# Token groups of 428, 426 and 426 in the down product, and all output blocks turned at its end

## The chip, the cores and the metric

One core of a Trainium2 chip runs the kernel. The metric is the device time of one execution in microseconds, the median of several runs. A profiled execution gives the span from the first to the last instruction, and what each engine did in it.

## The reference

One layer of a hybrid backbone works on 256 context tokens and 1024 latent tokens of 1024 features. After a recurrent branch and an attention branch comes a feed-forward part with a convolution along the tokens, then a last normalisation:

```python
def conv_ffn(h, lp):
    u, gte = jnp.split(h @ lp['w_ffn_up'], 2, axis=-1)
    u = dwconv3(u, lp['conv_ffn'])
    return (jax.nn.gelu(u) * gte) @ lp['w_ffn_down']

    x = x + g2 * conv_ffn(h2, lp)          # in layer(); g2 differs for context and latent tokens
    y_prompt = rmsnorm(xp, norm_f_g)       # in reference()
    y_sample = rmsnorm(xs, norm_f_g)
```

The change concerns the product with `w_ffn_down` (2816 x 1024, called the down product here), the gated addition to x, and the last normalisation. All is float32.

## The kernel before

Features lie on the 128 partitions and tokens along the free dimension; the 1280 tokens are stored with the 256 of the context first. Each float32 product is made of three matmuls of rounded parts (`split_mm`, L1069 to L1071): high part of the weights by high part of the tokens' values, high by low, low by high. The parts are made by the other engines: ScalarE rounds (`activation` with Copy), VectorE and GpSimd subtract the rounded from the whole.

The order of the work on each engine is written out by hand, with semaphores between the engines. The down product runs last. Its input, the gated hidden values (22 blocks of 128 features, `fact_kept`), and x1 (`x1_kept`) have been written to device memory before.

- `DOWN` (L630) lists three groups of tokens, as first token and count. For each group c the kernel goes through the 22 blocks of the hidden dimension; the step j = 22c + k holds 8 output blocks n of 3 matmuls each, 24 matmuls on 128 weights by the group's tokens. Each output block n accumulates over the 22 steps of a group in its own bank of PSUM (2 KB a partition, 512 float32 values); in the group of 256 two blocks share a bank, so that group uses banks 0 to 3 (`down_bank`).
- Operands of a step lie in a ring of three slots. SyncE (SP) loads a step's weights, 512 KB (`load_down`, L1012), and hidden values (`load_fact`, L1020) once PE has ended the step that was three earlier. ScalarE rounds the weights and then the tokens' values (L2215, L2216). GpSimd (POOL) splits the upper half of the weights (L3018); VectorE (DVE) splits their lower half (L2841) and then the tokens' values (L2844, `split_down`). PE waits for all of these (`down_part`).
- At the end of a group VectorE reads the eight banks, multiplies by the gate and adds x1 (`add_down`, L2854). In its own order this stands behind the split of the third step of the next group. PE's first step of a new group waits, block by block, for this add.
- An output block of 128 tokens is then turned by eight transposes on PE into a pair of banks (`turn_y`, L1741); ScalarE squares and sums it and takes the root of the mean (`square_y`, L2207 and L2209); VectorE takes the reciprocal and scales by it and by the gain (`scale_y`, L2860 and L2867) into one of four buffers; SP stores it (`store_y`, L1047). The groups run in the order tokens 256 to 767, 768 to 1279, 0 to 255. So eight of the ten output blocks are ready to be turned while the third group runs; they use banks 4 to 7 then, one in every second step (`y_step`). The last two follow the last add.

Of the kernel before, what the change touches and what calls it, by code (L numbers as in the profile page):

```python
# [22 lines left out]
P = 128  # L23
# [116 lines left out]
def build(nc, dram):  # L140
    ctx = ExitStack()
    with ctx:
# [487 lines left out]
        DOWN = [(256, 512), (768, 512), (0, 256)]  # L630
# [13 lines left out]
        Y_BLOCKS = list(range(2, TB)) + [0, 1]  # L644
# [49 lines left out]

        def y_step(q):

            return 2 * FB + 2 + 2 * q
# [18 lines left out]
        def _(sp):  # L716
# [327 lines left out]
            def store_y(q):  # L1044
                b = Y_BLOCKS[q]
                sp.wait_ge(y_ready, q + 1)
                sp.dma_start(dram["y"][b], y_tok[:, q % 4, :]).then_inc(tiles_moved[q % 4], 16)  # L1047

            for j in range(SLOTS, NSTEP):
                load_down(j)  # L1050
                load_fact(j)
                for q in range(TB - 2):
                    if j == min(y_step(q) + 5, NSTEP - 1):
                        store_y(q)
            for q in range(TB - 2, TB):
                store_y(q)
# [7 lines left out]
        def _(pe):  # L1064
# [643 lines left out]
            def down_bank(c, n):  # L1708

                if c < 2:  # L1710
                    return PS[:, n, 0:512]
                return PS[:, n // 2, 256 * (n % 2):256 * (n % 2) + 256]

            def down_part(j, blocks):

                c, k = j // FB, j % FB
                s, m = j % SLOTS, DOWN[c][1]
                pe.wait_ge(w_split, DOWN_SPLIT + j + 1)
                pe.wait_ge(fact_split, 2 * j + 2)
                for n in blocks:  # L1720
                    if k == 0 and c == 1:
                        pe.wait_ge(post_out, POST * FB + n + 1)
                    if k == 0 and c == 2:
                        pe.wait_ge(post_out, POST * FB + KB + n // 2 + 1)
                    ins = split_mm(down_bank(c, n), down_hi[s][:, n, :], down_lo[s][:, n, :],
                                   down_fH[s][:, 0:m], down_fL[s][:, 0:m], k == 0 and (c < 2 or n % 2 == 0),
                                   k == FB - 1 and (c < 2 or n % 2 == 1))
                    if k == FB - 1 and n < KB - 1:
                        ins.then_inc(w_used, 1)
                return ins  # L1730

            def turn_y(q):

                b = Y_BLOCKS[q]
                pe.wait_ge(post_out, POST * FB + KB * (3 if b < 2 else 1 if b < 6 else 2))
                if q == 0:
                    pe.wait_ge(post_out, POST * FB + 2 * KB)
                if q >= 2:
                    pe.wait_ge(y_ready, q - 1)
                for k in range(KB):  # L1740
                    ins = pe.transpose(PS[:, 4 + 2 * (q % 2) + k // 4, (k % 4) * P:(k % 4 + 1) * P],  # L1741
                                       x1_back[:, k, b * P:(b + 1) * P], ident)
                ins.then_inc(yt_done, 1)
# [7 lines left out]
            for j in range(1, NSTEP):  # L1751
                down_part(j, range(KB)).then_inc(w_used, 1)
                for q in range(TB - 2):
                    if j == y_step(q):
                        turn_y(q)
            for q in range(TB - 2, TB):
                turn_y(q)
# [3 lines left out]
        def _(act):  # L1761
# [438 lines left out]
            def square_y(q):  # L2200

                act.wait_ge(yt_done, q + 1)
                if q >= 1:
                    act.wait_ge(yss_ready, 2 * q)
                at = 4 + 2 * (q % 2)
                banks = PS[:, at:at + 2, :].rearrange("p a n -> p (a n)")
                act.activation(y_sq, banks, ACT.Square, accum_out=tstat[:, 0, q:q + 1]).then_inc(yss_ready, 1)  # L2207
                act.wait_ge(yss_ready, 2 * q + 1)
                act.activation(tstat[:, 1, q:q + 1], tstat[:, 0, q:q + 1], ACT.Sqrt, bias=eps_c[:, 0:1], scale=1.0 / D) \  # L2209
                    .then_inc(yss_ready, 1)  # L2210

            for j in range(NSTEP):
# [4 lines left out]
                for q in range(TB - 2):  # L2217
                    if j == min(y_step(q) + 3, NSTEP - 1):
                        square_y(q)
            for q in range(TB - 2, TB):  # L2220
                square_y(q)
# [3 lines left out]
        def _(dve):  # L2225
# [620 lines left out]
            def add_down(c):  # L2846
# [4 lines left out]
                for n in range(KB):  # L2851
                    dve.wait_ge(w_used, block_used(c, n if c < 2 else n | 1))
                    out = PS[:, n, 0:512] if c < 2 else PS[:, n // 2, 256 * (n % 2):256 * (n % 2) + 256]
                    stt(x1_back[:, n, t0:t0 + m], out, mod[:, 40 + n, int(c < 2):int(c < 2) + 1], x1_back[:, n, t0:t0 + m],  # L2854
                        ALU.mult, ALU.add).then_inc(post_out, 1)

            def scale_y(q):
# [7 lines left out]
                at = 4 + 2 * (q % 2)  # L2865
# [3 lines left out]
            for j in range(NSTEP):  # L2869
# [3 lines left out]
                for q in range(TB - 2):  # L2873
                    if j == min(y_step(q) + 3, NSTEP - 1):
                        scale_y(q)
            add_down(2)
            for q in range(TB - 2, TB):
# [233 lines left out]
```

## Time and profile before

| | us |
|---|---|
| median of 3 runs (lowest, highest) | 2367.15 (2361.28, 2369.21) |
| profiled execution | 2367.85 |
| its span | 2365.8 |
| PE busy in the span | 2184.1 (92%) |
| VectorE busy | 1446.5 (61%) |
| ScalarE busy | 828.9 (35%) |
| GpSimd busy | 826.3 (35%) |
| mean granted clock of TensorE | 0.973 of 2.4 GHz |

All times of the trace are counted from the span's start. PE's matmuls are pipelined: the time from one start to the next says what a matmul costs in a stream, and its own duration is longer than that. "Idle before, released by" names what ended a wait. The down product runs from 2013.1 to 2355.9; all before it is untouched by the change.

### The profile page before, as it was taken

The page shows a single profiled execution, that of the slowest core. Times are in us where ns is not written, and L with a number is a line of the kernel's source. Part 1 is how long each engine was busy: PE and PEld are TensorE (multiplying, and loading weights), DVE is VectorE, ACT ScalarE, POOL GpSimd, SP SyncE. Part 2 cuts the span into 40 slices and gives each one's busy share as a digit, 9 for nine tenths or more (in the row PEclk, how much of TensorE's full clock was granted, in tenths as well). Part 3 has the DMA queues.
Part 4 walks back from the last instruction along what each step waited for, and adds up shares of the span by engine and source line. Part 5 has one row for each costly group of instructions (what it writes and reads, how often), then busy time and mean ns, then how long its engine had stood idle before and what let it go on. Part 6 is the DMA issues. An engine that isn't in the chain of part 4 may idle for free. (4 is left out here: it accounts for less than half of the span.)

```text
span 2365.8 us, 53206 instructions
## 1 busy us (share of the span) xinstructions
PE 2184.1 (92%) x23068; PEld 1904.0 (80%) x23068; DVE 1446.5 (61%) x2189; ACT 828.9 (35%) x1379; POOL 826.3 (35%) x459
## 2 busy tenths in 40 slices
PE   5899999999999988899699994999999999998987
PEld 4676776888888878888388874999999999787877
DVE  5867735284676678965656239665656656444456
ACT  5345245334655533333500013322222222222234
POOL 1112111211111122222443442766767674332333
PEclk9899999999999999999899996999999999999999
DMA  8322301224677876764134120121211213543445
GB/s 315 120 84 77 112 11 41 104 80 124 191 188 199 214 216 195 208 192 139 58 113 178 71 107 18 59 87 59 76 70 59 87 59 111 199 147 120 147 153 194
DMA packets 243107, 294.73 MB, mean 125 GB/s; under 512 B 144896, under 2 KB 182656, under 8 KB 241280
## 3 DMA queue, kind: packets, MB, share of 16 engines
q1 hardware_dynamic: 217600, 289.32, 37.2%
q10 hardware_dynamic: 25344, 3.15, 0.9%
q8 instruction: 114, 1.87, 0.3%
q14 instruction: 49, 0.40, 0.1%
HBM read 215.73 MB, written 76.68 MB: 124 GB/s over the span
## 5 line engine op out<-in xcount | busy, mean ns | idle before, releaser
L1069 PE MATMUL PS<-buffer,buffer 128*128 128x320 f32 (+2 forms) x3152 | 1084.0, 344 | 90.1 <-DVE buffer L2725 21.4
L1070 PE MATMUL PS<-buffer,buffer 128*128 128x320 f32 (+2 forms) x3152 | 1069.9, 339 | 0.0
L1071 PE MATMUL PS<-buffer,buffer 128*128 128x320 f32 (+2 forms) x3152 | 1069.1, 339 | 0.0
L1069 PEld LDWEIGHTS PS<-buffer,buffer 128*128 128x128 f32 x3152 | 601.9, 191 | 165.6 <-issue 90.3
L1071 PEld LDWEIGHTS PS<-buffer,buffer 128*128 128x128 f32 x3152 | 601.5, 191 | 52.2
L1070 PEld LDWEIGHTS PS<-buffer,buffer 128*128 128x128 f32 x3152 | 602.9, 191 | 49.8 <-issue 1.0
L2998 POOL TENSOR_TENSOR buffer<-buffer,buffer 128x512 fp32r<-128x512 f32 x154 | 262.7, 1733 | 50.8 <-ACT buffer L2147 46.2
L3018 POOL TENSOR_TENSOR buffer<-buffer,buffer 128x512 fp32r<-128x512 f32 x66 | 117.5, 1782 | 249.4 <-ACT buffer L2215 249.4
L2920 POOL TENSOR_TENSOR buffer<-buffer,buffer 128x1024 fp32r<-128x1024 f32 x28 | 72.1, 2575 | 353.5 <-ACT buffer L1951 353.5
L2147 ACT ACTIVATE buffer<-buffer 128x512 fp32r<-128x512 f32 x110 | 69.1, 632 | 309.6 <-POOL buffer L2992 166.7
L2841 DVE TENSOR_TENSOR buffer<-buffer,buffer 128x512 fp32r<-128x512 f32 x66 | 48.9, 741 | 169.3 <-ACT buffer L2215 169.1
L2215 ACT ACTIVATE buffer<-buffer 128x1024 fp32r<-128x1024 f32 x66 | 69.9, 1059 | 231.6 <-DMA buffer<-fact_kept 231.6
L2929 POOL TENSOR_TENSOR buffer<-buffer,buffer 128x512 f32<-128x512 f32 x40 | 53.0, 1344 | 187.5 <-PE PS L1488 171.6
L2887 POOL TENSOR_TENSOR buffer<-buffer,buffer 128x1024 fp32r<-128x1024 f32 x12 | 28.5, 2374 | 243.0 <-DMA buffer<-in_w_in 199.2
L2844 DVE TENSOR_TENSOR buffer<-buffer,buffer 128x512 fp32r<-128x512 f32 (+1 forms) x66 | 108.1, 1637 | 0.0
L2907 POOL TENSOR_TENSOR buffer<-buffer,buffer 128x1024 fp32r<-128x1024 f32 x18 | 43.0, 2391 | 147.4 <-DMA buffer<-in_w_in 71.1
L2992 POOL TENSOR_TENSOR buffer<-buffer,buffer 128x512 f32<-128x512 f32 x66 | 86.4, 1310 | 17.4 <-PE PS L1071 14.1
L2802 DVE TENSOR_TENSOR buffer<-buffer,PS 128x320 f32<-128x320 f32 x44 | 21.5, 488 | 111.5 <-PE PS L1071 111.5
L2243 DVE CUSTOM_DVE_ANT_0 buffer<-buffer,buffer 128x1024 f32<-128x1024 f32 x64 | 80.4, 1256 | 13.9 <-DMA buffer<-in_w_ada 12.2
L2342 DVE TENSOR_REDUCE buffer<-buffer 128x1 f32<-128x640 f32 (+2 forms) x80 | 53.8, 681 | 46.2 <-ACT buffer L1833 46.1
L2992 POOL TENSOR_TENSOR buffer<-buffer 128x512 f32<-128x512 f32 x22 | 28.3, 1286 | 131.7 <-PE PS L1071 131.7
L2494 DVE TENSOR_TENSOR_SCAN buffer<-buffer,buffer 128x512 f32<-128x512 f32 x20 | 24.2, 1251 | 81.6 <-ACT buffer L1982 81.6
(254 smaller groups left out, 3027.9 us busy)
## 6 DMA issues: line engine op xcount, KB each, us to landing
buffer<-in_w_down SPq DMA_DIRECT2D x66, 512.0 KB, 3.4
buffer<-in_w_up SPq DMA_DIRECT2D x44, 512.0 KB, 3.9
buffer<-in_w_in SPq DMA_DIRECT2D x42, 512.0 KB, 4.9
ops_kept<-buffer SPq DMA_DIRECT2D x40, 512.0 KB, 5.1
buffer<-ops_kept SPq DMA_DIRECT2D x80, 256.0 KB, 3.3
buffer<-in_w_ada SPq DMA_DIRECT2D x32, 512.0 KB, 4.0
buffer<-rkv_kept SPq DMA_DIRECT2D x120, 128.0 KB, 3.6
fact_kept<-buffer SPq DMA_DIRECT2D x22, 640.0 KB, 2.9
```

Source lines behind the costliest of these rows:

```text
L1069: mm(out, w_hi, x_hi, start=start, stop=False)
L1070: mm(out, w_hi, x_lo, start=False, stop=False)
L1071: return mm(out, w_lo, x_hi, start=False, stop=stop)
L2147: act.activation(aH[name], src, ACT.Copy).then_inc(w_round, 1)
L2215: act.activation(down_hi[slot], down_w[slot], ACT.Copy).then_inc(w_round, 1)
L2243: return dve.tensor_tensor_reduce(spare, src, silu[:, c, :], 1.0, 0.0, ALU.mult, ALU.add, dst[:, c:c + 1])
L2342: dve.tensor_reduce(rowstat[:, t % 3, 0, h:h + 1], scr[t % 2][:, h, step_at(t):KEYS], AX.X, ALU.max, negate=True) \
L2844: tt(down_fL[slot][:, 0:m], down_f[slot][:, 0:m], down_fH[slot][:, 0:m], ALU.subtract).then_inc(fact_split, 1)
L2920: pool.tensor_tensor(lo[t % 2], raw[t % 2], hi[t % 2], ALU.subtract).then_inc(w_split, 1)
L2992: pool.tensor_tensor(out, x, y, op).then_inc(weights_summed, 1)
L2998: pool.tensor_tensor(aL[f % 2][name], whole, aH[name], ALU.subtract).then_inc(w_split, 1)
L3018: pool.tensor_tensor(down_lo[slot][:, 4:KB, :], down_w[slot][:, 4:KB, :], down_hi[slot][:, 4:KB, :], ALU.subtract).then_inc(w_split, 1)
```

## The change

The list of token groups becomes three of nearly equal size, in the order of the tokens: 0 to 427, 428 to 853, 854 to 1279. Each block of each group has its own bank. The first group spans the border between context and latent tokens at 256, where the gate differs, so its adds are two instructions per block, of 256 and of 172 columns. A wait of PE for an add is now for block n of the group before, in each of the later groups. No output block is turned within the down product: all ten follow the last add, in the order of the tokens, with four pairs of banks in turn in place of two; the waits of a turn for an earlier block's end reach four blocks back in place of two. ScalarE's squares, VectorE's scales and SP's stores move to the end in the same way.

```diff
-        DOWN = [(256, 512), (768, 512), (0, 256)]
+        DOWN = [(0, 428), (428, 426), (854, 426)]
...
-        Y_BLOCKS = list(range(2, TB)) + [0, 1]
...
-        def y_step(q):
-
-            return 2 * FB + 2 + 2 * q
...
             for j in range(SLOTS, NSTEP):
                 load_down(j)
                 load_fact(j)
-                for q in range(TB - 2):
-                    if j == min(y_step(q) + 5, NSTEP - 1):
-                        store_y(q)
-            for q in range(TB - 2, TB):
+            for q in range(TB):
                 store_y(q)
...
                 for n in blocks:
-                    if k == 0 and c == 1:
-                        pe.wait_ge(post_out, POST * FB + n + 1)
-                    if k == 0 and c == 2:
-                        pe.wait_ge(post_out, POST * FB + KB + n // 2 + 1)
-                    ins = split_mm(down_bank(c, n), down_hi[s][:, n, :], down_lo[s][:, n, :],
-                                   down_fH[s][:, 0:m], down_fL[s][:, 0:m], k == 0 and (c < 2 or n % 2 == 0),
-                                   k == FB - 1 and (c < 2 or n % 2 == 1))
+                    if k == 0 and c > 0:
+                        pe.wait_ge(post_out, POST * FB + KB * (c - 1) + n + 1)
+                    ins = split_mm(PS[:, n, 0:m], down_hi[s][:, n, :], down_lo[s][:, n, :],
+                                   down_fH[s][:, 0:m], down_fL[s][:, 0:m], k == 0, k == FB - 1)
...
             def turn_y(q):
 
-                b = Y_BLOCKS[q]
-                pe.wait_ge(post_out, POST * FB + KB * (3 if b < 2 else 1 if b < 6 else 2))
-                if q == 0:
-                    pe.wait_ge(post_out, POST * FB + 2 * KB)
-                if q >= 2:
-                    pe.wait_ge(y_ready, q - 1)
+                pe.wait_ge(post_out, POST * FB + KB * 3)
+                if q >= 4:
+                    pe.wait_ge(y_ready, q - 3)
                 for k in range(KB):
-                    ins = pe.transpose(PS[:, 4 + 2 * (q % 2) + k // 4, (k % 4) * P:(k % 4 + 1) * P],
-                                       x1_back[:, k, b * P:(b + 1) * P], ident)
+                    ins = pe.transpose(PS[:, 2 * (q % 4) + k // 4, (k % 4) * P:(k % 4 + 1) * P],
+                                       x1_back[:, k, q * P:(q + 1) * P], ident)
...
             for j in range(1, NSTEP):
                 down_part(j, range(KB)).then_inc(w_used, 1)
-                for q in range(TB - 2):
-                    if j == y_step(q):
-                        turn_y(q)
-            for q in range(TB - 2, TB):
+            for q in range(TB):
                 turn_y(q)
...
                 for n in range(KB):
-                    dve.wait_ge(w_used, block_used(c, n if c < 2 else n | 1))
-                    out = PS[:, n, 0:512] if c < 2 else PS[:, n // 2, 256 * (n % 2):256 * (n % 2) + 256]
-                    stt(x1_back[:, n, t0:t0 + m], out, mod[:, 40 + n, int(c < 2):int(c < 2) + 1], x1_back[:, n, t0:t0 + m],
-                        ALU.mult, ALU.add).then_inc(post_out, 1)
+                    dve.wait_ge(w_used, block_used(c, n))
+                    for a, b in ((t0, min(t0 + m, CTX)), (max(t0, CTX), t0 + m)):
+                        if a >= b:
+                            continue
+                        side = int(a >= CTX)
+                        ins = stt(x1_back[:, n, a:b], PS[:, n, a - t0:b - t0], mod[:, 40 + n, side:side + 1], x1_back[:, n, a:b],
+                                  ALU.mult, ALU.add)
+                        if b < t0 + m:
+                            V.step(ins)
+                        else:
+                            ins.then_inc(post_out, 1)
```

## Rows read from the trace of the kernel before

**Rows 1.** Waits, 2010 to 2366 us: waiter, releaser, total us, times, longest us.

```profile
PE PS L1069 <- DVE buffer L2854: 16.3, 2, 8.4
PE PS L1069 <- DVE buffer L2844: 13.7, 10, 7.0
```

**Rows 2.** Stretches: length, busy PE, PEld, DVE, ACT, POOL; clock, DMA share, GB/s.

```profile
2013.10:2143.60 130.50, 122.14 (x528) 100.70 (x529) 56.67 (x50) 34.77 (x44) 40.45 (x23) 0.96 0.46 162
2143.60:2273.30 129.70, 121.79 (x528) 100.41 (x529) 56.96 (x53) 34.13 (x44) 39.44 (x22) 0.97 0.38 131
2273.30:2352.80 79.50, 72.84 (x568) 71.00 (x569) 55.58 (x61) 37.59 (x63) 33.67 (x19) 0.95 0.61 210
```

**Rows 3.** PE's timeline: start, duration (us), instruction, idle before; the first matmuls of three steps.

```profile
2102.46 0.39 PE L1069 MATMUL PS<-buffer,buffer 128*128 128x512 f32 x1
...
2107.90 0.39 PE L1069 MATMUL PS<-buffer,buffer 128*128 128x512 f32 x1
...
2352.80 0.36 PE L1069 MATMUL PS<-buffer,buffer 128*128 128x256 f32 x1 [0.68 <-DVE buffer L2844]
```

**Rows 4.** The same, ends of two streams: 24 starts of 320, 20 of 256 columns.

```profile
1989.97 0.30 PE L1071 MATMUL PS<-buffer,buffer 128*128 128x320 f32 x1
...
1993.47 0.31 PE L1071 MATMUL PS<-buffer,buffer 128*128 128x320 f32 x1
...
2303.02 0.28 PE L1069 MATMUL PS<-buffer,buffer 128*128 128x256 f32 x1
...
2305.42 0.28 PE L1071 MATMUL PS<-buffer,buffer 128*128 128x256 f32 x1
```

**Rows 5.** Stretches behind two starts, PE alone: length, busy, clock, DMA share, GB/s.

```profile
2013.10:2017.80 4.70, 4.67 (x11) 0.50 0.97 418
...
2143.60:2147.50 3.90, 3.89 (x9) 0.50 0.00 0
```

**Rows 6.** The chain that ended last, first change of group: start, us, what.

```profile
2135.67 3.67 DMA buffer<-fact_kept
...
2139.36 1.06 ACT buffer L2215
...
2141.05 1.75 DVE buffer L2844
2142.80 0.67 DVE buffer L2854
```

**Rows 7.** Groups by shape (busy us, mean ns, idle before); last adds in the chain.

```profile
L2844 DVE TENSOR_TENSOR buffer<-buffer,buffer 128x256 fp32r<-128x256 f32 x22 | 32.1, 1457 | 0.0
...
L2854 DVE SCALAR_TENSOR_TENSOR buffer<-PS,buffer,buffer 128x256 f32<-128x256 f32 x8 | 3.2, 475 | 1.1 <-PE PS L1071 1.1
...
2353.80 3.24 DVE buffer L2854 x8
```

**Rows 8.** VectorE's timeline: the tokens' split of the first group's fourth step.

```profile
2029.24 1.78 DVE L2844 TENSOR_TENSOR buffer<-buffer,buffer 128x512 fp32r<-128x512 f32 x1
```

**Rows 9.** Loads at L1020, 2273 to 2352 us, from issue to landing.

```profile
DMA to landing us min/median/max: 3.3/3.6/5.4
```

**Rows 10.** Timeline of the end: start, duration (us), instruction, idle before.

```profile
2355.63 0.28 PE L1071 MATMUL PS<-buffer,buffer 128*128 128x256 f32 x1
2357.08 1.97 PE L1741 MATMUL PS<-buffer,buffer 128*128 128x128 f32 x16 [1.16 <-DVE buffer L2854]
2358.20 1.02 ACT L2207 ACTIVATE buffer<-PS 128x1024 f32<-128x1024 f32 x1 [7.39 <-PE PS L1741]
...
2359.74 1.02 ACT L2207 ACTIVATE buffer<-PS 128x1024 f32<-128x1024 f32 x1
...
2361.41 1.28 DVE L2867 SCALAR_TENSOR_TENSOR buffer<-PS,buffer,buffer 128x1024 f32<-128x1024 f32 x1
```

**Rows 11.** ScalarE's timeline: the one load of an activation table in the product.

```profile
2290.06 1.28 ACT L2209 ACT_TABLE_LOAD   x1
```

**Rows 12.** DMA issues, 2357 to 2365.8 us: count, KB each, median us to landing.

```profile
out_y<-buffer SPq DMA_DIRECT2D x2, 512.0 KB, 2.6
```

More of the change, by code:

```diff
@@ L1044, in store_y @@
             def store_y(q):
-                b = Y_BLOCKS[q]
                 sp.wait_ge(y_ready, q + 1)
-                sp.dma_start(dram["y"][b], y_tok[:, q % 4, :]).then_inc(tiles_moved[q % 4], 16)
+                sp.dma_start(dram["y"][q], y_tok[:, q % 4, :]).then_inc(tiles_moved[q % 4], 16)
             for j in range(SLOTS, NSTEP):
@@ L1706, in _ @@
                         ins.then_inc(w_used, 1)
[L1708 to L1712, printed above, removed]
             def down_part(j, blocks):
@@ L1732, in turn_y @@
             def turn_y(q):
-                b = Y_BLOCKS[q]
-                pe.wait_ge(post_out, POST * FB + KB * (3 if b < 2 else 1 if b < 6 else 2))
-                if q == 0:
-                    pe.wait_ge(post_out, POST * FB + 2 * KB)
-                if q >= 2:
-                    pe.wait_ge(y_ready, q - 1)
+                pe.wait_ge(post_out, POST * FB + KB * 3)
+                if q >= 4:
+                    pe.wait_ge(y_ready, q - 3)
                 for k in range(KB):
-                    ins = pe.transpose(PS[:, 4 + 2 * (q % 2) + k // 4, (k % 4) * P:(k % 4 + 1) * P],
-                                       x1_back[:, k, b * P:(b + 1) * P], ident)
+                    ins = pe.transpose(PS[:, 2 * (q % 4) + k // 4, (k % 4) * P:(k % 4 + 1) * P],
+                                       x1_back[:, k, q * P:(q + 1) * P], ident)
                 ins.then_inc(yt_done, 1)
@@ L2204, in square_y @@
                     act.wait_ge(yss_ready, 2 * q)
-                at = 4 + 2 * (q % 2)
+                at = 2 * (q % 4)
                 banks = PS[:, at:at + 2, :].rearrange("p a n -> p (a n)")
@@ L2216, in _ @@
                 act.activation(down_fH[slot][:, 0:m], down_f[slot][:, 0:m], ACT.Copy).then_inc(fact_rounded, 1)
[L2217 to L2220, printed above, removed]
+            for q in range(TB):
                 square_y(q)
@@ L2864, in scale_y @@
                     dve.wait_ge(tiles_moved[q % 4], 64 + 16 * (q // 4))
-                at = 4 + 2 * (q % 2)
+                at = 2 * (q % 4)
                 banks = PS[:, at:at + 2, :].rearrange("p a n -> p (a n)")
@@ L2872, in _ @@
                     add_down(j // FB - 1)
-                for q in range(TB - 2):
-                    if j == min(y_step(q) + 3, NSTEP - 1):
-                        scale_y(q)
             add_down(2)
-            for q in range(TB - 2, TB):
+            for q in range(TB):
                 scale_y(q)
```

## The prediction

> **What bounds the kernel now.** Four views were read, in this order.
>
> First the waits of TensorE (PE) inside the down product [rows 1]. PE waits there for VectorE only: two long waits for the adds that clear the banks (L2854), and ten for the split of a step's operands (L2844), the longest of them at the start of the product.
>
> Then the busy time by token group [rows 2]. The two groups of 512 tokens take 130.50 and 129.70 us up to the next group's first matmul, and PE is busy for 122.14 and 121.79 of it. The group of 256 takes 79.50 us to the start of its last step, with 72.84 busy and the DMA engines at 0.61 in place of 0.38.
>
> Then the timeline of PE. A step of 512 tokens is 24 matmuls and takes 5.44 us, start to start (2102.46 to 2107.90), 226.7 ns each [rows 3]. In the group of 256 twenty matmuls start within 2.40 us [rows 4], 120 ns each; the times are in hundredths of a microsecond, and I take 119.5, a step of 2.87 us. So a group of 512 is 22 x 5.44 = 119.7 us of matmuls, and the rest of it is a start at the half clock and a stall. The granted clock is 0.50 (1.2 in place of 2.4 GHz) for 4.70 us after the first start and for 3.90 us after the second [rows 5]; half of it is lost each time, 2.3 and 1.95 us. What is left is the stall at the change of group: 130.5 - 119.7 - 2.3 = 8.5 us and 129.7 - 119.7 - 1.95 = 8.1 us.
>
> The group of 256 would be 22 x 2.87 = 63.1 us of matmuls. It took 79.5 + 2.9 = 82.4. The surplus of 19.3 us is eight turns, about 0.87 us each in the chain of work (6.9), the half clock at its start (1.95), and waits for operands together with a second stretch at the half clock (the remaining 10.4). The reason is the ring of three slots: step j can load only when step j-3 has ended, and load, rounding and split then have two steps to hide behind, 5.7 us where the steps have 256 tokens. By the chain of one such load (landing 3.67, rounding 1.06, 0.63 to the tokens' split, 1.75 for it, and some 0.5 for the two issues) it takes about 7.6 us [rows 6]. Solved for group three, whose 21 steps took 79.5 us: three average steps are 11.4 us, so the loop there, with stores in its way, took 11.4 - 2.9 = 8.5.
>
> Last the end [rows 10]: matmuls end at 2355.91, the adds at 2357.04, and two turned blocks pass ScalarE, VectorE and a store until 2365.8. ScalarE begins a block each 1.54 us.
>
> **The change, part by part.**
>
> *Columns.* The same 1584 matmuls and the same 1280 tokens per output block stay. From 512 and 256 columns (226.7 and 119.5 ns) the line has 0.419 ns per column; at 320 columns it gives 146.3, and the trace has 24 starts in 3.50 us, 145.8 [rows 4]. So 428 columns are 191.5 ns and a step 4.60 us, 426 are 190.7 and 4.58. Groups: 22 x 4.60 + 44 x 4.58 = 302.7 us against 2 x 119.7 + 63.1 = 302.5. **+0.2 us**: the even split gains nothing in the array itself.
>
> *Group three.* Its steps last 4.58 us, so the loop of a slot has 9.16 us against 7.6 to 8.5: no waits inside. The eight turns leave too. Only the half clock at its start stays, 2.0 us as in group two. **-17.3 us** (19.3 less 2.0).
>
> *The first group's fourth step.* Here the cover gets thinner. The first start is at 2013.1 [rows 2], and about 0.05 earlier after the change. The step's operands came late: the tokens' split began at 2029.24 and took 1.78, to 2031.02, because x1 (5 MB), the gain and the last factor block are being moved, with the DMA engines at 0.97 [rows 5, 8]; PE needed it at 2013.1 + 2.3 + 3 x 5.44 = 2031.7. With steps of 4.60 PE needs it at 2013.05 + 2.3 + 3 x 4.60 = 2029.15. The same bytes must pass before it, so I let it be ready only 0.2 us earlier (a smaller load and a shorter split), and with 0.1 to the matmul at 2030.95: **+1.8 us**. If its earlier issue (about 1.1 us) counted in full it would be 0.8, and with other traffic out of the way nothing; the range takes 0 to 2.5.
>
> *The two changes of group.* Nothing overlaps there before or after: end of step 21, load, rounding, split, first add, first matmul [rows 6]. First change: the tokens' split lies between 1.75 (512) and 1.46 (256), about 1.66; the load has a tenth fewer bytes; the first add is now two instructions, 256 columns and 172. In the chain an add of 256 takes 0.40 (eight in 3.24 us) and one of 512 takes 0.67, 1.04 ns a column, so 172 take 0.32, the pair 0.72 and 426 columns 0.58 [rows 6, 7]. 8.5 becomes 8.4. Second change: its split was the short one of 256 and becomes 1.66, the add 0.58 in place of 0.67: 8.1 becomes 8.2. **0 us**; bounds -0.5 and +1.0 for both, by the scatter of the landings. Adding c = 0 costs VectorE 0.72 us a block against 1.07 of PE at the half clock (three matmuls of 428 at 357 ns), 0.57 at the full one, so PE doesn't overtake the adds in its first eight blocks. What queues behind the adds on VectorE is the split of step 25, whose load is not issued before step 22 has ended.
>
> *The end.* Eight turns move behind the last add. From the end E of the last matmul: the blocks end 0.57 us apart, an add of 426 follows its neighbour at 0.58 and by itself lasts 0.65 (475 ns at 256 columns), so the last add ends at about E + 0.8 (before: 1.13). The first turn gives ScalarE its start 1.12 us later as before (2357.08 to 2358.20). Ten blocks then follow at 1.54 us, and the last one needs from its start 2365.8 - 2359.74 = 6.06 us, square, root, scale and store [rows 10]. The square and root of the first block had a table load between them, 1.28 us, which lay under matmuls at 2290.06 [rows 11]; it comes with the first root and now lies on the path. Sum: 0.8 + 1.12 + 1.28 + 9 x 1.54 + 6.06 = 23.1 us against 9.9 before: **+13.2 us**. Are the other stages faster than ScalarE? PE turns a block in 0.87 at full clock and may run three blocks ahead, since there are four pairs of banks now; VectorE needs 1.28 for its scale [rows 10] and about 0.1 for a reciprocal; a store of 512 KB lands 2.6 us after issue [rows 12], and the ring of four blocks allows 4 x 1.54 - 1.28 = 4.9. So 1.54 holds; 2.0 per block (the margin of every stage used up) would add 4.1, and nothing in the trace would make it shorter than 1.4 (-1.3).
>
> The Trainium skill speaks of the table load, in "ScalarE: Activation LUTs", What ACT_TABLE_LOAD costs: a load of about 1283 ns and a drain of about 1380 ns at each switch. The row has the first, and the root starts 0.01 us behind it with no drain to be seen. By the page the end would be 1.4 us longer; the row decides.
>
> *SP's queue.* The ten stores no longer stand between loads in group three, where a store held the next load behind it at most by its issue (0.34 us). Part of the 17.3.
>
> *Start.* The first step's split of 428 tokens is 0.1 us shorter.
>
> **Sum against the profiled execution** (span 2365.8, time 2367.85): +0.2 - 17.3 + 1.8 + 0 + 13.2 - 0.1 = -2.2; laid out along the timeline, with the roundings kept (2013.05 + 113.7 + 110.95 + 98.1 + 27.9), the end is at 2363.7, **-2.1 us**. That profiled execution lay 0.7 over the median of the runs, 2367.15. Forecast: 2367.15 - 2.1 = **2365.1 us**.
>
> **The rivals.** A change of 0.3%, 7.1 us, is about what a measurement of this kernel tells from none.
>
> *A, slower: uneven widths cost more.* Every long stream in the trace has 256, 320 or 512 columns. If a matmul of 428 or 426 cost as much as one of 448, it would be 20 x 0.419 = 8.4 or 22 x 0.419 = 9.2 ns more, 528 x 8.4 + 1056 x 9.2 = 14.1 us: 2379. Rounding up to 432 would cost 3.5 us and change no verdict. It decides from (7.1 + 2.1) / 1584 = 5.8 ns a matmul. For it: no row excludes it. Against it: 256, 320 and 512 lie on one line within 0.5 ns.
>
> *B, slower: the loop of a slot stays the bound.* If load to split took over 9.16 us, each step would last (C + 4.58) / 3. For it: landings of 5.4 us were seen in group three [rows 9], in place of 3.7. Against it: they were those between the stores, which are gone from there. A loop of 10 us would give 0.28 x 60 = +17 us: 2382. It decides from 9.6 us.
>
> *C, slower but within the bound: the turns at the end run at the half clock.* PE pauses between them now. A turn would be 1.74 us, over ScalarE's 1.54. The first would start the chain 0.87 later, and the three blocks of lead are spent by about the tenth: +1 to +2 us, 2366.6. In the trace the sixteen turns at the end ran within 1.97 us, at the full clock [rows 10].
> The Trainium skill, "TensorE: Matmul & The Clock Gate", Part 4: PE-mode transpose, says that transposes in the engine's transpose mode don't count as activity for the clock in the way that matmuls do, which speaks against moving them together. By that rule the case is C.
>
> *D, faster.* The fourth step doesn't stall (-1.8), the half clock after each stall is a little shorter (0.3 us of loss less each time: -1), and the loads at the two changes of group land at 3.3 and not 3.7 (-0.8): 2361.5. It takes a favourable draw of the clock more to get past 7.1 us.
>
> **How the numbers follow.** Forecast with C and the favourable draws that stay within 7.1 us: 0.70 (C alone about 0.15 of that). A 0.08, B 0.05, other slips on the slow side, such as an end at over 2 us a block together with a stall at the fourth step, 0.04: slower 0.17. D with a draw beyond: faster 0.13. The range: below, D and 2 us of scatter of a median, 2359.5; above, the forecast with 4.1 for the end, 1 for the group changes, 0.7 for the fourth step and about 2 of scatter, 2373.0. A and B lie outside it, with 0.13, and some 0.05 below it.
>
> **What the profile after would show.** Twenty-four starts in 4.60 and 4.58 us; one wait of about 1.8 us at the first group's fourth step and no other inside any group; two of about 8.3 us at the group changes; the half clock three times for 4 to 5 us of matmuls; last matmul at about 2340.6; ten squares 1.54 us apart, and a table load behind the first. The prediction is wrong in its first step if a step of 428 isn't 4.60 us, in its largest if steps of group three wait, and in its second largest if the squares are further apart than 1.54 us.

## The result

The changed kernel takes 2374.87 us (median of 14 runs, 2368.37 to 2380.66) against 2366.72 us before in the same runs (2361.28 to 2372.26): a ratio of 1.0036, with a 95% interval of 1.0026 to 1.0047. It is slower by about 8 us, clear of the noise and outside the range that was forecast.

The stretches of the profile after, cut where those of [rows 2] are (length, busy PE, PEld, DVE, ACT, POOL; clock, DMA share, GB/s):

```profile
2012.90:2132.20 119.30, 107.81 (x529) 103.71 (x529) 54.50 (x51) 33.20 (x44) 40.18 (x23) 0.93 0.51 175
2132.20:2246.30 114.10, 105.90 (x528) 101.79 (x529) 56.01 (x60) 33.19 (x44) 39.53 (x22) 0.96 0.44 144
2246.30:2346.70 100.40, 100.37 (x504) 96.86 (x505) 47.65 (x45) 28.67 (x38) 34.17 (x19) 0.98 0.43 141
2346.70:2374.60 27.90, 16.26 (x105) 14.66 (x104) 19.25 (x28) 15.38 (x31) 0.00 (x0) 0.85 0.47 188
```

The third group now waits for nothing: 100.37 us busy in 100.40, where [rows 2] have 72.84 in 79.50. The last stretch, from the start of the last step, is 27.90 us against 13.0, and 27.9 was the forecast. The first group is the one that is off: 119.30, with 11.5 us in which PE stands, where 113.7 had been laid out. PE's waits (waiter, releaser, total us, times, longest), beside [rows 1]:

```profile
PE PS L1060 <- DVE buffer L2830: 16.6, 2, 8.4
PE PS L1060 <- DVE buffer L2817: 8.8, 2, 5.7
```

The two waits for adds are as before. The second line holds the wait at the product's start and a new one, on the first group's fourth step. Its first matmul, and the granted clock behind it and behind the three group starts (timeline and stretches, PE alone):

```profile
2032.73 0.70 PE L1060 MATMUL PS<-buffer,buffer 128*128 128x428 f32 x1 [3.10 <-DVE buffer L2817]
...
2012.90:2018.20 5.30, 5.28 (x15) 0.51 0.95 410
2032.70:2038.30 5.60, 5.57 (x16) 0.50 0.06 21
2132.20:2137.20 5.00, 5.00 (x14) 0.50 0.00 0
2246.30:2250.00 3.70, 3.67 (x10) 0.50 0.00 0
```

The half clock (1.2 GHz) comes four times up to the last group, not three; a fifth stretch, in the turns at the end, is read below under rival C. The spacing of steps of 24 matmuls, one pair of starts in the first group and one in the second, as in [rows 3]:

```profile
2058.70 0.36 PE L1060 MATMUL PS<-buffer,buffer 128*128 128x428 f32 x1
...
2063.34 0.36 PE L1060 MATMUL PS<-buffer,buffer 128*128 128x428 f32 x1
...
2205.08 0.35 PE L1060 MATMUL PS<-buffer,buffer 128*128 128x426 f32 x1
2209.78 0.35 PE L1060 MATMUL PS<-buffer,buffer 128*128 128x426 f32 x1
```

4.64 us, not 4.60; and with 426 columns 4.69 (on average 4.693), not 4.58. The narrower matmul is the dearer one here. The price of 428 columns isn't one number, though. The first group's second step, before the pause and at the full clock, took 4.70 us:

```profile
2020.06 0.35 PE L1060 MATMUL PS<-buffer,buffer 128*128 128x428 f32 x1
...
2024.76 0.36 PE L1060 MATMUL PS<-buffer,buffer 128*128 128x428 f32 x1
```

The account of the two profiled executions, from the first matmul of the product to the end (352.7 us before, 361.7 after). A step of 256 columns counts 2.88 us in it, 24 times the 120 ns of [rows 4], where the prediction took 2.87:

| term | forecast | measured |
|---|---|---|
| columns: all steps at the full clock | +0.2 | 308.6 - 302.7 = +5.9 |
| third group: turns, waits, half clock inside | -17.3 | 1.8 - 19.1 = -17.2 |
| first group's fourth step: wait, and half clock behind it | +1.8 | 3.3 + 2.8 = +6.1 |
| changes of group (8.5 and 8.4 after; 8.5 and 8.1 before) | 0 | +0.3 |
| half clock at the starts of groups one and two (2.6 and 2.5 after; 2.3 and 2.0 before) | 0 | +0.8 |
| end, from the last matmul | +13.2 | 23.0 - 9.9 = +13.1 |
| sum | -2.1 | +9.0 |

### The profile page after: what moved, and what is told of

Its sections match the earlier page's. It is cut to its first block and busy times, and to the rows that moved or that the text cites. A ratio compares the mean times of both kernels' runs of the same rounds, so it can differ in the third digit from the quotient of the medians.

```text
span 2374.6 us, 53211 instructions
## 1 busy us (share of the span) xinstructions
PE 2192.1 (92%) x23068; PEld 1945.6 (82%) x23068; DVE 1449.8 (61%) x2197; ACT 830.3 (35%) x1379; POOL 827.8 (35%) x459
## 5 line engine op out<-in xcount | busy, mean ns | idle before, releaser
L1060 PE MATMUL PS<-buffer,buffer 128*128 128x320 f32 (+4 forms) x3152 | 1085.8, 344 | 85.3 <-DVE buffer L2698 20.3
L1062 PE MATMUL PS<-buffer,buffer 128*128 128x320 f32 (+4 forms) x3152 | 1072.7, 340 | 0.0
L1061 PE MATMUL PS<-buffer,buffer 128*128 128x320 f32 (+4 forms) x3152 | 1072.3, 340 | 0.0
L2817 DVE TENSOR_TENSOR buffer<-buffer,buffer 128x426 fp32r<-128x426 f32 (+1 forms) x66 | 108.3, 1641 | 0.0
L2969 POOL TENSOR_TENSOR buffer<-buffer,buffer 128x512 f32<-128x512 f32 x66 | 86.4, 1311 | 17.3 <-PE PS L1062 14.0
L2216 DVE CUSTOM_DVE_ANT_0 buffer<-buffer,buffer 128x1024 f32<-128x1024 f32 x64 | 80.4, 1256 | 13.9 <-DMA buffer<-in_w_ada 12.2
```

Of the source, the lines that this page charges most:

```text
L1060: mm(out, w_hi, x_hi, start=start, stop=False)
L1061: mm(out, w_hi, x_lo, start=False, stop=False)
L1062: return mm(out, w_lo, x_hi, start=False, stop=stop)
L2216: return dve.tensor_tensor_reduce(spare, src, silu[:, c, :], 1.0, 0.0, ALU.mult, ALU.add, dst[:, c:c + 1])
L2817: tt(down_fL[slot][:, 0:m], down_f[slot][:, 0:m], down_fH[slot][:, 0:m], ALU.subtract).then_inc(fact_split, 1)
L2969: pool.tensor_tensor(out, x, y, op).then_inc(weights_summed, 1)
```

## The experiments

### Which widths cost more

The seven kernels of this part with other widths were executed once each, so only the spacing of their matmuls is read, not their times.

**Three kernels with other widths.** The one edit, for the first:

```diff
-        DOWN = [(0, 428), (428, 426), (854, 426)]
+        DOWN = [(0, 448), (448, 416), (864, 416)]
```

> The changed kernel with groups of 448, 416 and 416 tokens. Measured so far: a matmul of 512, 320 and 256 columns takes 13 ns more than its columns at 2.4 GHz, one of 428 takes 15.0 and one of 426 takes 18.0 ns more. Theory 1 (the surplus hangs on the width being a multiple of something that 448, 416, 512, 320 and 256 all are, 32 or less): 448 columns 199.9 ns, a step of 4.80 us; 416 columns 186.5 ns, a step of 4.48 us; all steps 302.7 us in place of 308.6, so some 5.9 us less than the changed kernel. Theory 2 (a surplus that varies smoothly with the width and is highest about 430, or belongs to the changed kernel and not to the width): 416 and 448 near 15 to 18 ns over their columns too, steps of 4.86 and 4.56 us.

> The changed kernel with groups of 432, 424 and 424 tokens. Theory 1 with 16 as the unit: 432 is like 512 (193.2 ns, a step of 4.64 us), 424 (a multiple of 8 alone) has a surplus like 428 or between it and 13 ns: 189.9 to 191.7 ns, a step of 4.56 to 4.60 us. With 8 as the unit 424 has 13.2 ns, 4.56 us. Theory 2 (smooth): 424 has 18 ns as its neighbour 426, a step of 4.67 us, and 432 about 15, 4.68 us.

> The changed kernel with groups of 428, 428 and 424 tokens. If width alone decides, the first two groups have steps of 4.64 us as the first group of the changed kernel, and the third has what 424 has in the run with 432, 424, 424. If the surplus belongs to the place in the product (second and third group) and not to the width 426, the second group's 428 columns take more than 4.64 us.

Steps were 4.864 and 4.52 us (448 and 416 columns), 4.70 and 4.64 (432, 424), and 4.64, 4.64 and 4.64 (428, 428, 424). The last says that the place in the product doesn't set the price of 428 columns: in the second group they are as in the first. The first kills theory 1: 448 and 416 are multiples of 32 and have 16 and 15 ns of surplus. Of theory 2, 424 with 16.7 ns stays near its neighbour 426.

**512 first, then 384.** `DOWN = [(0, 512), (512, 384), (896, 384)]`, nothing else.

> The changed kernel with groups of 512, 384 and 384 tokens. Columns: 512 should keep 226.7 ns (5.44 us a step) although it now stands first and the kernel is the changed one; if 384 has the 13 ns of 256, 320 and 512, its step is 4.16 us, if it has the 15 to 16.7 ns seen from 416 to 448, 4.20 to 4.24 us. The fourth step: the first group's longer steps give its operands 2.4 us more, so it waits 0 to 1 us and not 3.3.

The steps are 5.44 and 4.16 us: both have 13.3 ns, so the surplus of 15 to 18 ns does not belong to the changed kernel whatever its widths, nor to a bank used by one block alone. Two step starts of its second group:

```profile
2191.24 0.33 PE L1060 MATMUL PS<-buffer,buffer 128*128 128x384 f32 x1
...
2195.40 0.33 PE L1060 MATMUL PS<-buffer,buffer 128*128 128x384 f32 x1
```

The fourth step waited 0.6 us. With more time before it the wait shrinks, by 2.7 us where 2.4 were expected.

**480 and 400.**

> The changed kernel with groups of 480, 400 and 400 tokens. So far the surplus of a matmul over its columns at 2.4 GHz is 13.3 ns at 256, 384 and 512 columns, and 15.0 (416), 16.7 (424), 18.0 (426), 15.0 (428), 15.8 (432), 16.0 (448). If 13.3 belongs to multiples of 128, both widths have more, 15 to 16: steps of 5.16 to 5.18 and 4.36 to 4.38 us. If the surplus is a hump between 384 and 512 with its top near 426, both lie between: 400 near 14 ns (4.34 us), 480 near 14.5 ns (5.15 us). If multiples of 16 or 32 have a rule of their own, 480 is as 448 (16.0, 5.18 us) and 400 as 432 (15.8, 4.38 us).

```profile
2071.90 0.38 PE L1060 MATMUL PS<-buffer,buffer 128*128 128x480 f32 x1
...
2077.10 0.38 PE L1060 MATMUL PS<-buffer,buffer 128*128 128x480 f32 x1
...
2188.75 0.34 PE L1060 MATMUL PS<-buffer,buffer 128*128 128x400 f32 x1
...
2193.07 0.34 PE L1060 MATMUL PS<-buffer,buffer 128*128 128x400 f32 x1
```

5.20 and 4.32 us: 480 has 16.7 ns, 400 has 13.3. None of the three theories gives both.

**408, 464, 392, 496, and the changed kernel once more.**

> The changed kernel with groups of 408, 408 and 464 tokens. A weight load lasts 188 ns in the trace at every width. Up to 400 columns (a start every 180 ns) the loads leave no gap and the surplus is 13.3 ns; at 424 and more (193 ns and up) there are gaps between the loads. Theory (the surplus rises where the time from one start to the next comes near and passes the 188 ns of a load): 408 columns, 183 ns, still have about 13.3 (4.40 us a step), 464 have 16 to 17 (5.04 us). Rival (a rule by width: multiples of 16 are good except some): 408 has 15 to 17, 464 is as 400.

> The changed kernel with groups of 496, 392 and 392 tokens. By the weight load's 188 ns: 392 has 13.3 ns of surplus though it is a multiple of 8 alone (4.24 us a step); 496 lies between 480 (16.7) and 512 (13.3), about 15 (5.32 us). By a rule of multiples of 16: 392 has more than 14, 496 is as 512 (5.28 us).

> The changed kernel as it is, once more. The first group's 428 columns took 193.3 ns in four kernels (4.64 us a step) and 196 ns in a fifth that differs from them on VectorE alone (4.70). If the pitch of a width is fixed, the steps are 4.64 and 4.69 us again; if a group falls into one of several rhythms at its start, 428 columns may show 4.70 here. The time: 1.0036 of the kernel before, as measured.

408 and 464 columns had steps of 4.44 and 5.04 us (15.0 and 16.7 ns), 496 and 392 had 5.36 and 4.256 (16.7 and 14.0). The duration of a weight load as a threshold falls: 408 is already dearer at 185 ns from start to start, under the 188, and 512, the furthest above it, is back at 13.3.

The changed kernel gave 4.64 and 4.69 us again, 1.0029 of before (1.0014 to 1.0044), and again a fourth step with 3.3 us of wait and 2.8 at the half clock. Its second step took 4.70 us again too. So 428 columns have two rhythms, and they can follow each other in one group of one execution: starts 191, 194, 201, 195, 199 ns apart, over and over, in the first steps, and 193, 193, 194 ns behind the pause. In the run of 428, 428 and 424, and in the one with the load of x1 moved (below), 428 columns had 4.64 us from the second step on. In the one with the adds ahead of both splits (below) they kept 4.70 through the whole group, a pause of 2.7 us included. The width alone doesn't fix the spacing; what picks the rhythm is not known. The groups of 426 columns had 4.69 in every one of the ten seen.

All widths together, as nanoseconds of a matmul over its columns at 2.4 GHz:

| columns | surplus | columns | surplus |
|---|---|---|---|
| 256, 320, 384 | 12.5 to 13.3 | 428 | 15.0, in the other rhythm 17.5 to 17.8 |
| 392 | 14.0 | 432 | 15.8 |
| 400 | 13.3 | 448 | 16.0 |
| 408, 416 | 15.0 | 464, 480, 496 | 16.7 |
| 424 | 16.7 | 512 | 13.3 |
| 426 | 18.0 | | |

It is a plateau of 15 to 18 ns between 408 and 496, with lower ground on both sides. Why is open: neither a multiple of the width nor the weight load's duration explains it, nor, for 428, the place.

### The third group and its ring

**The turns alone moved to the end**, in the kernel before, with its 512, 512 and 256:

```diff
             for j in range(1, NSTEP):
                 down_part(j, range(KB)).then_inc(w_used, 1)
-                for q in range(TB - 2):
-                    if j == y_step(q):
-                        turn_y(q)
-            for q in range(TB - 2, TB):
+            for q in range(TB):
                 turn_y(q)
```

and the same for squares, scales and stores, with four pairs of banks.

> The kernel before with its groups of 512, 512 and 256, but with all ten output blocks turned after the last add, through four pairs of banks as in the changed kernel. My theory: the third group is bound by the loop of a slot (load, rounding, split, 7.6 us, and one step), not by the turns, so its steps without turns and stores take (7.6 + 2.87) / 3 = 3.5 us, 77 us for the group in place of 82.4, and the end takes 13.2 us more: 7.8 us slower than the kernel before. Rival: the turns and stores are what slows the third group, and without them it takes 63.1 + 2 = 65 us: 4 us faster than before.

Measured 1.0061 of before (1.0044 to 1.0078), some 14 us slower. The third group without any turn (same columns as [rows 2]):

```profile
2273.90:2350.70 76.80, 66.61 (x504) 64.32 (x504) 44.61 (x45) 25.94 (x38) 33.96 (x19) 0.95 0.51 163
```

76.80 us for 21 steps against 79.50. Eight turns and their eight stores less brought 2.7 us; the group still waits for its operands, 3.66 us a step against 3.5 expected and 2.9 of work. The rival is out. In the profile the kernel is 12.2 us slower from the first matmul to the end (364.9 us), where 7.8 had been expected: 2.7 of the miss are in the third group, 1.2 in the end, 27.4 us from the last step's start, where 26.2 had been reckoned, and 0.5 in a fourth step that was late here. The turns and the waits lie over each other: taking away only the turns, 6.9 us in the prediction's sum, gave 2.7.

**Four slots in place of three**, in the kernel before (`SLOTS = 4`, the buffers behind moved up by a block, the fourth slot's first load behind the product whose input lay there).

> The kernel before (512, 512, 256, turns in the third group) with four slots for a step's operands in place of three. Theory (the third group is bound by the loop of a slot): with three steps to hide behind (8.6 us) against a load to split of about 8.1, its steps take 2.9 us and those with a turn 3.7, 72 us for the group in place of 82.4; at each change of group the load of the third step is issued one step earlier, so PE stands about 3 us in place of 8.3. Some 20 us less than before, 0.991 to 0.993. Rival (the third group is bound by the DMA engines' rate or by VectorE, which has 1.45 us splits, adds and scales in 2.9 us steps): the third group stays at 80 us, and only the changes of group gain, 0.996.

0.9916 of before (0.9887 to 0.9944), 2347.2 us. The third group:

```profile
2263.20:2330.60 67.40, 67.40 (x569) 67.40 (x570) 53.67 (x61) 37.49 (x63) 32.14 (x19) 1.00 0.74 242
```

PE is busy in all 67.40 us, with the turns inside and the DMA engines at 0.74 in place of 0.61. The same work with one more step of cover has no wait: what slowed the group of 256 was the loop of a slot. Its matmuls still take 120 ns here.

### The fourth step

**The load of x1 in pieces, later.**

```diff
-            sp.dma_start(x1_back.rearrange("p k t -> p (k t)"), dram["x1_kept"]).then_inc(stage_out[1], 16)
-            sp.dma_start(gain_f, dram["norm_f"].to_broadcast([P, D])).then_inc(consts_in, 16)
             keep_fact(FB - 1)
...
             for j in range(SLOTS, NSTEP):
                 load_down(j)
                 load_fact(j)
+                if SLOTS < j <= SLOTS + 2 * KB:
+                    load_x1(j - SLOTS - 1)
...
```

`load_x1` loads half of one of the eight feature blocks; the gain's load follows the last piece, and VectorE's first add waits for all sixteen.

> The changed kernel, with the load of x1 (5 MB) cut into 16 pieces that are issued one behind each of the loads of steps 4 to 19, and the gain's load behind them. In the changed kernel step 3 (the fourth) waited 3.3 us for its operands and then ran 2.8 us longer at the half clock. Theory (the load of x1 stands before the operands of step 3 in the DMA engines): its landing falls from 8.6 to about 4 us, no wait at step 3, 6 us less than the changed kernel: about 1.001 of the kernel before. Rival (the load is late for another reason, its own issue or the store of the last factor block): the wait stays, and the time stays at 1.0036.

1.0013 of before (1.0000 to 1.0025). The landing of the fourth step's hidden values in the changed kernel, and here:

```profile
DMA to landing us min/median/max: 8.6/8.6/8.6
```

```profile
DMA to landing us min/median/max: 3.8/3.8/3.8
```

Step 3 (the fourth) follows step 2 at 4.64 us without a gap, the clock doesn't fall, and from the first matmul to the end the profile is 6.5 us shorter (355.2 for 361.7).

### The changes of group

**The adds ahead of the third step's split**, in the changed kernel:

```diff
-                if j % FB == 2 and j >= FB:
+                if j % FB == 1 and j >= FB:
                     add_down(j // FB - 1)
```

> The changed kernel, with VectorE's adds of a finished group moved ahead of the split of the next group's third step (they stood behind it). Theory: the 8.4 us in which PE stands at each change of group are the load, rounding and split of that third step, which the adds wait for only by their order on VectorE. Without it PE waits for the first add alone, about 0.9 us each, and if so short a pause leaves the clock up, the 2.5 and 1.8 us at the half clock go too: 15 to 19 us less than the changed kernel, 0.995 to 0.997 of the kernel before. Rival: PE needs the split of the third step by then anyhow, or the adds (0.58 to 0.72 us a block against 0.59 of PE) hold it back block by block: 5 us or less.

0.9982 of before (0.9968 to 0.9996). It helped less than expected: 3.8 and 3.6 us were left at the changes. The chain of work there (start, us, what):

```profile
2116.02 0.33 SPq L1007
...
2116.39 3.63 DMA buffer<-fact_kept
...
2120.05 1.07 ACT buffer L2191
...
2121.74 1.66 DVE buffer L2817
2123.41 0.71 DVE buffer L2830 x2
```

The load at its head is issued at 2116.02, at the start of the group's last step: it is that of the second step of the next group. The adds stood behind the wrong split still.

**Ahead of both splits** (`j % FB == 0`).

> The changed kernel, with the adds of a finished group ahead of the splits of both the second and the third step of the next group. The run with the adds ahead of the third step's split alone still had 3.7 us between the last matmul of a group and the first of the next, not the 0.9 expected. Theory: there the adds stood behind the split of the second step, whose load is issued one step (4.65 us) before the group's end and takes 7.6 us; ahead of it PE waits 0.9 us, and without a long pause the clock stays up at both changes. 5.5 us less than that run, and 2.5 more for the clock of the second group: 0.995 to 0.996 of the kernel before. Rival: the adds themselves, or the banks' turn from reading to writing, take the 3.7 us; then nothing changes.

0.9944 of before (0.9927 to 0.9961): 9 us less than the run before it. Not 0.9 us are left at a change but nothing: 4.70 and 4.69 us from the last step's start to the next group's first, with the clock up, and 0.4 us more in the second group's first two steps: a bank is needed only when its own block comes round, seven blocks after it was finished, and its add has ended by then. Its 428 columns took 4.70 us a step all through the group; at 4.64 it would be 1.4 us better.

**Four slots and early adds**, in the kernel before, with the groups of 512, 512 and 256 and the turns inside the third.

> The kernel before with four slots (0.9916, a wait of 2.96 and 2.52 us at the changes of group), and with the adds ahead of the split of the next group's third step. With four slots the second step's operands are loaded two steps before the group's end, 10.9 us against 7.6, so the adds wait for no load: 0.9 us at each change of group, 3.8 us less, 0.990 of the kernel before. If the rule were another, it stays at 0.9916.

0.9876 of before (0.9859 to 0.9893), 2336.8 us: 30 us faster than the kernel before and 38 than the changed one. PE's waits by the same view as at the top:

```profile
PE PS L1071 <- DVE buffer L2846: 8.0, 2, 7.8
PE PS L1743 <- DVE buffer L2856: 1.2, 1, 1.2
```

What is left is the product's start (7.8) and the last add. The long waits for adds are gone from the list.

### The sum again, without the two terms that failed

Groups of 512, 384 and 384 and the x1 load in pieces: the 6 us of the width and the 6 us of the fourth step are both taken out of the changed kernel, and all else of it stays.

> The changed kernel with groups of 512, 384 and 384 tokens (13.3 ns surplus in all, as measured) and with the load of x1 in 16 pieces behind the loads of steps 4 to 19. Theory (the prediction failed in two terms only, the width's price of 6 us and the fourth step's wait with its half clock, 6 us): both are gone, all steps take 302.7 us, and the time is the prediction's sum without its 1.8 us for the fourth step, 2.1 + 1.8 = 3.9 us below the kernel before: 0.9984. Rival (something else of the changed kernel costs time too, in the end or at the changes of group): 1.000 or above.

0.9993 of before, interval 0.9984 to 1.0002. Theory and rival lie at the two ends of it, so the times don't part them; the profile does. From first matmul to end it takes 350.4 us against 352.7, 2.2 less, where 3.9 had been reckoned. Of the 1.7 that are missing, 1.6 lie in small things that can be read there: 0.6 us more at the half clock after the three starts, a few steps 0.04 to 0.14 us long (0.3 together), 0.2 at the changes of group, and 0.5 in the end, where 3.65 us pass from the end of the last scale to the end of the last store in place of 3.09 in the changed kernel. No third cause of several us is hidden in the changed kernel.

## Why the prediction was wrong

It was wrong in sign and missed by 10 us. In the profiles the miss is 11.1 us, and two terms make 10.0 of it, 5.7 and 4.3, both on the same side. The rest is 0.8 us more at the half clock behind the first two starts, a term that the prediction kept as it was, and 0.3 at the changes of group.

**"The even split gains nothing in the array itself", +0.2 us.** This is the step that failed first. It drew a line through 256, 320 and 512 columns and read 428 and 426 off it. Both lie in a stretch, 408 to 496, where every width tried is above that line: 1.8 ns at 428 and 4.9 ns at 426, 528 x 1.8 + 1056 x 4.9 = 6.1 us (5.9 in the account above, which counts the 256 columns of before with their 120 ns; the line was drawn from 119.5). Rival A was this mechanism with the wrong form. It asked whether the price would be that of 448, 8 to 9 ns; such rounding isn't there, for 424 costs what 428 does, and 426 more than both. It said that the verdict turns from 5.8 ns a matmul. Alone the width stayed below that, 3.9 ns on average, and together with the next term it didn't need to reach it. That rival's evidence against (three widths on one line) was no evidence for the space between the last two.

**"The first group's fourth step", +1.8 us, range 0 to 2.5.** The place and the cause were right: shorter steps, the same bytes in front. The size was not. PE was ready for the step at 2029.4, near the 2029.15 forecast. The operands were to be ready 0.2 us earlier than before and were so 1.6 us later (2032.6 in place of 2031.0), because the load of x1 had itself been issued 1.2 us later than in the trace of before, and all queued behind it. The issue of x1 before, then the issue and the step's last split after:

```profile
2006.12 0.32 SPq L1040 DMA_DIRECT2D buffer<-x_kept  x1
...
2007.30 0.32 SPq L1035 DMA_DIRECT2D buffer<-x_kept  x1
...
2030.91 1.67 DVE L2817 TENSOR_TENSOR buffer<-buffer,buffer 128x428 fp32r<-128x428 f32 x1
```

In all fifteen traces with x1 in one load this split ends 24.6 to 25.4 us behind that load's issue (before 24.9, after 25.3), while the issue itself lies 5.6 to 7.8 us before the product's first matmul. So the term hung on a time that differs from one kernel and execution to the next, by more than its own size. And the second half of the price wasn't in the working at all: a pause of 3.1 us let the clock fall again, 2.8 us more. The prediction had counted the half clock at the two changes of group and the start, where it is in both kernels, and not at the one wait that it added itself. In the seven other traces with a first group of 408 to 448 columns and the x1 load in its old place, the wait was 2.2 to 3.6 us and the half clock behind it cost 0.1 to 2.9.

**Right within 0.3 us:** the third group (-17.3, -17.2), the changes of group, and the end (+13.2, +13.1), with the squares 1.54 us apart from the second on and the table load of 1.28 us behind the first. That the third group's number came out doesn't show its parts: it was right because waits, turns and stores all went at once (see the turns alone). The stores that left it were eight, not ten. In the chain of work after:

```profile
2353.46 1.11 ACT buffer L2183 x2
2354.59 1.28 ACT L2185
2355.88 0.30 ACT buffer L2185
...
2356.27 1.12 ACT buffer L2183 x2
...
2357.80 1.12 ACT buffer L2183 x2
```

The root starts 0.01 us behind the table load here too, so the drain that the Trainium skill's "ScalarE: Activation LUTs" adds to a switch (What ACT_TABLE_LOAD costs) isn't on this path.

**Rival B** (the slot's loop stays the bound) didn't come: no wait inside groups two and three. **Rival C** (turns at the half clock) came for two blocks and cost nothing. The changed kernel's sixth and seventh blocks' transposes ran at the half clock, 213 ns from start to start in place of 109 and 1.7 us a block, as rival C has it (stretches in front of, in and behind them, PE alone):

```profile
2357.80:2359.00 1.20, 1.06 (x8) 1.00 0.39 157
2359.50:2362.60 3.10, 3.10 (x16) 0.50 0.87 348
2362.80:2364.00 1.20, 1.08 (x10) 0.97 0.81 324
```

These two blocks were turned 1.2 and 1.0 us before ScalarE took them up, so the squares stayed 1.54 us apart. The half clock comes in these turns in six of the fourteen traces with ten turns at the end. Here it came behind pauses of 1.8 and 0.5 us with eight transposes between them, and left while PE ran transposes alone. The Trainium skill, "TensorE: Matmul & The Clock Gate", Part 4: PE-mode transpose, has it that transposes don't count for the clock as matmuls do; the return to 1.00 behind these sixteen transposes, with nothing but transposes on the engine since 2352.33, doesn't agree with that, and the rule had no price here.

**Rival D** had the sign of its first two parts wrong: the wait and the half clock both grew.

**The chances.** "Within 0.3%" had 0.70. The measured change, 0.36% with an interval from 0.26 to 0.47, lies just beyond that bound, which its interval takes in; "slower" had 0.17. What made 0.70 too much is that both failed terms had more room on the slow side: three widths on one line left little to gain, and the fourth step could give back its 1.8 us at most.

## What to carry to other kernels

Before groups are made even, ask why the narrow one is slow. Here it was a ring with too few slots, and a fourth slot took 20 us where even groups, moving the covered work to the end, could win 4 at most. A matmul's price at one width is known from streams of that width and not from a line between others; and a wait of a few us that a change adds on TensorE can have a second price, the stretch at the half clock behind it (here 0.1 to 2.9 us). Where an engine stands at a change of stage, look for what its releaser did last in its own order: moving one add loop by two places in VectorE's program took away 16 us of waits.

## What the runs showed of the hardware that had not been expected

- float32r streams (three matmuls of parts, each with its own weights) cost 13.3 ns over N/2.4 GHz at N = 384, 400 and 512, and 15 to 18 ns at every width tried from 408 to 496. 424 and 428 columns cost the same 193.3 ns; 426 cost 195.6. The numbers repeated in a second run of the same program. 428 columns also ran at 196 ns, in the changed kernel's own first steps and, in a program that differs on VectorE alone, for a whole group. The cause is open.
- A pause of TensorE of 3.1 us was followed by 5.6 us at the half clock, a loss of 2.8 us (stretch of 2032.7 above). At the same place in the other traces pauses of 2.1, 2.7 and 2.9 us cost 0.1 us behind them, pauses of 2.6 and 2.9 cost 1.5, one of 3.5 cost 2.9. With the adds ahead of the third step's split, a pause of 3.5 us at the second change of group cost 0.1, and one of 3.6 at the first cost 2.4. So the length of the pause alone doesn't tell the price.
- The clock can come back during transposes alone: in the changed kernel 16 of them ran at a granted clock of 0.50, 213 ns apart, and the next ones at the full clock, 109 ns apart.
- A load of 214 KB took 8.6 us to land behind 5 MB, and 3.8 us without them.
